# First four chunks normed while modulation blocks load, two attention units made inside the transform, turned head outputs in the head products' bank

## The chip, the cores and the metric

The kernel runs on one core of a Trainium2 chip. The metric is the device time of one execution, in microseconds (us), the median of several. Engines are named as in the profile: TensorE (PE, and PEld for its weight loads), VectorE (DVE), ScalarE (ACT), GpSimd (POOL), and SyncE (SP), which issues all transfers. Each engine works through its own instructions in order; semaphores order them against each other.

## The reference

Two layers of a diffusion backbone on 512 latent and 256 context tokens of width 1024, all in float32. Cut to what matters here:

```python
mod_x = silu(c) @ w_ada[l] + b_ada[l]          # nine vectors of 1024: shift, scale, gate of three sublayers
def ffn_sublayer(s, m, i, g, wg, wu, wd):
    h = rmsnorm(s, g) * (1 + m[3*i+1]) + m[3*i]
    return s + 0.5 * m[3*i+2] * ((silu(h @ wg) * (h @ wu)) @ wd)
# a layer: ffn_sublayer, then token mixing with u = h @ w_in, then ffn_sublayer
p = softmax(q @ k.T / 8)                        # 4 heads, two maps each
o = rmsnorm((p[0] - lam * p[1]) @ v) * const    # differential attention, latent queries see all keys
y = concat(o, conv_module(u), fourier_mix(u)) @ w_out
```

Here conv_module is gated, convolved over 31 tokens, LayerNormed, swished and mapped; fourier_mix is the real part of a 2-D DFT and a linear map. The last layer has no context output.

## The kernel before

**Layout.** Activations stand transposed: eight chunks of 128 channels by 768 tokens. A product is made of three (h_hi with w_hi, h_lo with w_hi, h_hi with w_lo), so each normed chunk h and each weight tile is split into a high part (ScalarE) and a low part (VectorE) before TensorE can use it. PSUM has eight banks. A class Plan numbers every product (slot), gives it a bank, the next in turn unless one is named, and counts each bank's uses; an engine waits for the number of a product, and TensorE (wait_bank, wait_freed) for the count of releases of the bank (bank_free).

**Start.** SyncE loads the tokens, then modulation weights in blocks of 512 columns (load_ada, two halves of 1 MB each), then weight tiles. Block 0 and 1 hold the first shift, 2 and 3 the first scale, for channel chunks 0 to 3 and 4 to 7; 4 and 5 hold the first gate. A block is sixteen matmul records (L1176), a copy by ScalarE (part, L1711), a turn into columns (turn, L1189) and a copy to mod by VectorE (L2157). In `ada(BEFORE)` blocks 0 to 3 come first on each engine, with the turned vectors and the norm's statistics between them. Then shift_scale makes the scales of all chunks and scaled (L2139, tn), high (L1688, h_hi) and low (L2150, h_lo) make the chunks, the context's (segment 1) ahead of the latent ones (segment 0). The up tile is split behind the first context chunk. gate_up_first runs the first group's passes: context gate, context up, blocks 4 and 5 (BETWEEN), then the latent passes.

**Mixing.** After the key, conv, query, value and Fourier projections, `fourier(l)` on TensorE makes the small products of the transform: mean of the convolution (L1451), DFT over positions Z (L1503), variance (L1460), spread of the scales (L1470), DFT over channels F (L1515), Fourier output Fo (L1523) and pointwise output pw (L1482). GpSimd makes the scales (conv_scales) between variance and spread. Fo and pw leave their banks when VectorE has made their low parts (L2710).

**Attention.** Its units are (head, segment, 128 queries): 24 in layer 0 (four latent and two context units a head), 16 latent ones in layer 1. A latent unit takes two of three pairs of banks 0 to 5. In step i TensorE does, in this order: the turn of head output i-9 (turn_o, L1390), the score of unit i (L1558), the first turn of the probabilities of unit i-2 (turn_p, L1572), the head product of unit i-3 (L1584, bank 7), the second turn of probabilities. Turned probabilities and turned head outputs both use bank 6. ScalarE in its step makes the exponents (L2008) and copies turned probabilities (L1994) and head outputs (L2024). VectorE does in step i:

```python
head_low(i - OT_LAG)    # low part of the turned head output, frees its bank
maximum(i)
combine(i - 1)          # the two maps of unit i-1 into one
take_o(i - O_LAG)       # copy of head product i-3 out of bank 7, frees it
```

In three steps each engine also splits a weight tile (1.9 us on ScalarE, 2.3 on VectorE). The last projection (out) follows, and in layer 0 one side product (modulation of a later sublayer) stands behind the first score.

## Time and profile before

| | us |
|---|---|
| median of 3 runs | 2696.61 (2695.8 to 2697.26) |
| the profiled execution | 2699.22 |
| its span, first to last instruction | 2697.4 |
| TensorE busy in it | 2587.2 (96%) |
| VectorE busy | 2079.5 (77%) |
| ScalarE busy | 1020.3 (38%) |
| mean granted TensorE clock, share of full | 0.987 |

TensorE sets the time nearly everywhere. A busy share is an average over stages: the waits by engine and source line tell where TensorE stands idle, and the timelines what it waited for. In a timeline row the columns are start, duration, engine, line, operation, output and inputs, tile shape and count, and in square brackets the idle time ahead of it and what ended it. One fp32 matmul of the start, transform or attention leaves two records.

### The profile page before, as it was taken

Reading aid. Unit: us, or ns where it says so; the run is one execution under the profiler, and the core shown is the slowest. Engines: PE = TensorE matmul, PEld = TensorE weight load, DVE = VectorE, ACT = ScalarE, POOL = GpSimd, SP = SyncE. Lnnn points to the kernel's source line nnn. Section 1 sums busy time; section 2 is a strip of 40 time slices with the busy share of each in tenths; the row PEclk is TensorE's granted clock in tenths of the full one; section 3 lists DMA queues with packets and bytes.
Section 4 is the critical chain, followed back from the end, with each engine's and each line's share of the span. In section 5 each row is a group of like instructions: output and inputs, shape, how many; then the busy total and the mean of one; then the engine's idle time right before and its main releaser. Section 6 shows DMA issues by size and latency. Waiting matters only on the chain. (4 is left out here: it accounts for less than half of the span.)

```text
span 2697.4 us, 42701 instructions
## 1 busy us (share of the span) xinstructions
PE 2587.2 (96%) x15352; PEld 2375.4 (88%) x15352; DVE 2079.5 (77%) x3420; ACT 1020.3 (38%) x1873; POOL 167.6 (6%) x316
## 2 busy tenths in 40 slices
PE   6999999999997999999999999999999987999998
PEld 4899999988955789999999799999997955889997
DVE  5698888888937478888888887777768856688886
ACT  4333432333147333332332434323324155344443
POOL 2000000020003210000000200000001013100001
PEclk7999999999999999999999999999999999999999
DMA  8134333332211112333334133333322211223331
GB/s 304 40 125 130 117 93 115 119 98 63 89 39 48 32 55 89 123 94 113 124 97 133 55 102 117 94 125 108 114 67 89 76 47 32 76 82 110 104 109 53
DMA packets 193241, 256.33 MB, mean 95 GB/s; under 512 B 7262, under 2 KB 130764, under 8 KB 193100
## 3 DMA queue, kind: packets, MB, share of 16 engines
q1 hardware_dynamic: 193100, 254.43, 29.5%
q8 instruction: 91, 1.49, 0.2%
q14 instruction: 50, 0.41, 0.0%
HBM read 252.31 MB, written 2.10 MB: 94 GB/s over the span
## 5 line engine op out<-in xcount | busy, mean ns | idle before, releaser
L1132 PE MATMUL ps<-h_hi,w_hi 128*128 128x384 f32 (+2 forms) x2368 | 792.3, 335 | 21.9 <-DVE h_lo L2150 19.4
L1134 PE MATMUL ps<-h_hi,w_lo 128*128 128x384 f32 (+2 forms) x2368 | 786.8, 332 | 0.0
L1133 PE MATMUL ps<-h_lo,w_hi 128*128 128x384 f32 (+2 forms) x2256 | 750.3, 333 | 0.0
L1132 PEld LDWEIGHTS ps<-h_hi,w_hi 128*128 128x128 f32 x2368 | 450.4, 190 | 54.1 <-issue 21.8
L1134 PEld LDWEIGHTS ps<-h_hi,w_lo 128*128 128x128 f32 x2368 | 450.4, 190 | 20.8
L1133 PEld LDWEIGHTS ps<-h_lo,w_hi 128*128 128x128 f32 x2256 | 429.0, 190 | 19.6 <-issue 1.0
L1663 ACT ACTIVATE w_hi<-raw 128x512 fp32r<-128x512 f32 x464 | 279.8, 626 | 419.1 <-PE ps L1134 325.8
L2282 DVE TENSOR_TENSOR w_lo<-raw,w_hi 128x512 fp32r<-128x512 f32 x464 | 307.3, 684 | 14.7 <-ACT w_hi L1663 14.7
L1132 PE MATMUL ps<-t_hi_all,w_hi 128*128 128x384 f32 x864 | 292.0, 338 | 0.0
L1134 PE MATMUL ps<-t_hi_all,w_lo 128*128 128x384 f32 x864 | 292.0, 338 | 0.0
L1133 PE MATMUL ps<-t_lo_all,w_hi 128*128 128x384 f32 x864 | 291.9, 338 | 0.0
L2205 DVE SCALAR_TENSOR_TENSOR side_acc<-side_raw,ccol,side_acc 128x512 f32<-128x512 f32 x364 | 258.0, 744 | 8.0 <-DMA side_raw<-in_w_ada 8.0
L2400 DVE SCALAR_TENSOR_TENSOR xT<-ps,gate,xT 128x384 f32<-128x384 f32 (+3 forms) x400 | 180.7, 503 | 83.6 <-PE ps L1134 83.4
L1124 POOL TENSOR_TENSOR sqsum<-sqsum,sq 128x256 f32<-128x256 f32 (+1 forms) x98 | 99.1, 1014 | 2027.5 <-ACT sq L1672 2021.0
L1663 ACT ACTIVATE w_hi<-w_sum 128x512 fp32r<-128x512 f32 x216 | 133.4, 626 | 229.3 <-DVE w_sum L866 121.6
L1132 PE MATMUL ps<-even_hi_all,w_hi 128*128 128x384 f32 (+2 forms) x576 | 197.7, 343 | 2.2 <-DVE even_lo_all L2379 2.2
L1134 PE MATMUL ps<-even_hi_all,w_lo 128*128 128x384 f32 (+2 forms) x576 | 195.2, 339 | 0.0
L1133 PE MATMUL ps<-even_lo_all,w_hi 128*128 128x384 f32 (+2 forms) x576 | 194.4, 337 | 0.0
L2282 DVE TENSOR_TENSOR w_lo<-w_sum,w_hi 128x512 fp32r<-128x512 f32 x216 | 147.5, 683 | 19.3 <-ACT w_hi L1663 19.3
L1133 PEld LDWEIGHTS ps<-t_lo_all,w_hi 128*128 128x128 f32 x864 | 162.2, 188 | 0.0
L1132 PEld LDWEIGHTS ps<-t_hi_all,w_hi 128*128 128x128 f32 x864 | 162.2, 188 | 0.0
L1134 PEld LDWEIGHTS ps<-t_hi_all,w_lo 128*128 128x128 f32 x864 | 162.2, 188 | 0.0
(257 smaller groups left out, 4039.5 us busy)
## 6 DMA issues: line engine op xcount, KB each, us to landing
side_raw<-in_w_ada SPq DMA_DIRECT2D x240, 256.0 KB, 2.7
raw<-in_w_ffn_gate SPq DMA_DIRECT2D x44, 1024.0 KB, 5.4
raw<-in_w_ffn_up SPq DMA_DIRECT2D x44, 1024.0 KB, 5.4
raw<-in_w_ffn_down SPq DMA_DIRECT2D x44, 1024.0 KB, 5.0
raw<-in_w_in SPq DMA_DIRECT2D x14, 1024.0 KB, 5.3
ada_buf<-in_w_ada SPq DMA_DIRECT2D x12, 1024.0 KB, 12.7
raw<-in_w_out SPq DMA_DIRECT2D x8, 1024.0 KB, 5.1
raw<-in_w_in SPq DMA_DIRECT2D x8, 512.0 KB, 6.7
```

Source lines behind the costliest of these rows:

```text
L1124: nc.gpsimd.tensor_tensor(sqsum[:, o:o + n], sqsum[:, o:o + n], sq[:, j % 2, o:o + n], ALU.add)\
L1132: mm(out, wh, xh, start=start, stop=False, skip_group_check=reopened)
L1133: mm(out, wh, xl, start=False, stop=False, skip_group_check=reopened)
L1134: return mm(out, wl, xh, start=False, stop=stop, skip_group_check=reopened)
L1663: act_fn(ring_part(w_hi, key(g)), part_source(key(g)), ACT.Copy).then_inc(w_hi_done, 1)
L2205: ins = stt(out=side_acc[:, v, :], in0=side_raw[k % 2][:], scalar=c, in1=side_acc[:, v, :], op0=ALU.mult, op1=ALU.add)
L2282: tt(ring_part(w_lo, key(g)), part_source(key(g)), ring_part(w_hi, key(g)).bitcast(F), ALU.subtract)\
L2400: ins = stt(out=xT[:, j, o:o + n], in0=ps[:, bank_of(key(x)), at_:at_ + n], scalar=gate[:, f // 2, i, j, v:v + 1], in1=xT[:, j, o:o + n], ...
```

## The change

It does three things.

1. **Start.** The blocks come in the order 0, 2, 1, 3. SyncE loads block 0, the constants, the first gate tile, then blocks 2, 1 and 3. TensorE makes block 0, the turned vectors, the statistics and block 2, then the gate passes of the context's chunks 0 to 3, then blocks 1 and 3 with their turns, then the latent chunks 0 to 3. VectorE splits the gate tile ahead of the reciprocals, and makes scales and chunks in two halves (`first_scale`, not shown below: adds the bias to, and makes the scale of, four chunks). The remaining gate passes and the up passes follow in `gate_up_begun`; the up tile is split late, behind latent chunk 5 on ScalarE and behind all chunks on VectorE.
2. **Transform.** Scores 0 and 1 of each layer are products of `fourier(l)`: score 0 and layer 0's side product ahead of the mean, score 1 behind the variance. The transform's other products take turns in banks 4 to 7; both early units use banks 0 to 3. Their maxima, exponents and the first combine move there too. Buffers for probabilities, the scales' diagonals and small columns get other places in SBUF. The attention begins with step 2.
3. **Attention.** Turned head outputs use bank 7, that of the head products, in place of bank 6.

```diff
@@ -74,8 +75,9 @@
-FIRST_BLOCKS = (0, 1, 2, 3, 4, 5)
-BEFORE, BETWEEN = FIRST_BLOCKS[:4], FIRST_BLOCKS[4:]
+FIRST_BLOCKS = (0, 2, 1, 3, 4, 5)
+BETWEEN = FIRST_BLOCKS[4:]
+EARLY = KD // 2
...
@@ -150,7 +152,8 @@
     for i, (h, s, t) in enumerate(units_of(l)):
         mine = [(n + k) % 3 for k in range(2 if s == 0 else 1)]
-        n += len(mine)
+        if i != EARLY_UNITS - 2:
+            n += len(mine)
         out.append((mine, max(busy_until[x] for x in mine)))
...
+    def first_ada(self):
+
+        self.tile(("G", 0, 0))
+        for kind in ("ada", "adaT"):
+            self.slot((kind, 0, 0))
+        for i in range(3):
+            self.slot(("vec", i))
+        for s in seg_order(0):
+            self.slot(("stat", 0, s))
+        for kind in ("ada", "adaT"):
+            self.slot((kind, 0, 2))
+
+        for n, key in enumerate((("ada", 0, 1), ("adaT", 0, 1), ("ada", 0, 3), ("adaT", 0, 3))):
+            self.slot(key, (self.bank + 4 + n) % 8)
...
@@ -330,7 +337,10 @@
+        rest = [(w, f, 0, c, second) for c in range(2) for w in "gu"]
+        if f == 0:
+            passes, rest = [(w, f, 0, c, s) for w in "gu" for s in (first, second) for c in range(2)], []
+        for key in passes + rest:
...
@@ -404,36 +419,43 @@
+        self.before_scores.append(list(self.uses))
+        banks = itertools.cycle(range(4, 8))
+
+        def place(*key):
+            self.slot(key, next(banks))
+
+        self.score(l, 0)
+        if l == MIX_SIDE[0] // 2:
+            place("side", *MIX_SIDE)
...
             if j == 0:
-                self.slot(("var", l))
+                place("var", l)
+                self.score(l, 1)
...
         for kind in ("Fo", "pw"):
             for p in range(2):
                 for s in range(ns):
-                    self.slot((kind, l, p, s))
+                    place(kind, l, p, s)
...
         u = units_of(l)
         self.before_att.append(list(self.uses))
         for i in attention_steps(l):
             if 0 <= i - OT_LAG < len(u):
-                self.slot(("OT", l, i - OT_LAG), 6)
+                self.slot(("OT", l, i - OT_LAG), 7)
             if i < len(u):
-                self.slots[("score", l, i)] = (self.n, None, None)
-                self.n += 1
-            if (l, i) == (0, 0):
-                self.slot(("side",) + MIX_SIDE, 6)
+                self.score(l, i)
...
-            for b in BEFORE[:3]:
+            for b in FIRST_BLOCKS[:1]:
...
             load(("G", 0, 0))
-            for half in range(2):
-                load_ada(3, half)
+            for b in FIRST_BLOCKS[1:4]:
+                for half in range(2):
+                    load_ada(b, half)
...
             def ada(blocks):
+                for b in blocks:
+                    ada_block(b)
+                for b in blocks:
+                    turn(b)
+
+            def first_pass(w, s, ks):
+
+                o, n = PIECES[s][:2]
+                wh, wl = wk((w.upper(), 0, 0), KD)
+                for k in ks:
+                    wait_h(0, k, s)
+                    for c in range(2):
+                        key = (w, 0, 0, c, s)
+                        if k == 0:
+                            wait_bank(pe, key)
+                        last = mm3(pt(key, n), wh[:, k, 128 * c:128 * c + 128], wl[:, k, 128 * c:128 * c + 128],
+                                   h_hi[:, k, o:o + n], h_lo[:, k, o:o + n], k == 0, k == KD - 1, True)
+                        if k == KD - 1:
+                            last.then_inc(products, 1)
+
+            def first_ada():
+                ada_block(0)
+                turn(0)
+                pe.wait_ge(const_landed, 16 * 3)
+                turn_vector(0)
+                turn_vector(1)
+                pe.wait_ge(taps_landed, 16)
+                turn_vector(2)
+                for s in seg_order(0):
+                    stat(0, s)
+                ada_block(2)
+                turn(2)
+                wait_split(("G", 0, 0))
+                first, second = seg_order(0)
+                first_pass("g", first, range(EARLY))
+                ada_block(1)
+                turn(1)
+                ada_block(3)
+                turn(3)
+                first_pass("g", second, range(EARLY))
...
+                def gate_up_begun():
+
+                    for w in "gu":
+                        if w == "u":
+                            wait_split(("U", 0, 0))
+                        for s in seg_order(0):
+                            first_pass(w, s, range(EARLY if w == "g" else 0, KD))
+                            if (w, s) == ("u", seg_order(0)[0]):
+                                ada(BETWEEN)
...
+                for b in range(4):
+
+                    pe.wait_ge(bank_free[b], plan.before_scores[l][b])
+                score(l, 0)
+                if l == MIX_SIDE[0] // 2:
+                    side_product(MIX_SIDE[0], lambda x: x, MIX_SIDE[1])
...
                     if j == 0:
                         conv_var()
+                        score(l, 1)
                 conv_spread()
...
+            def score(l, i):
+
...
-                for b in range(6):
+                for b in (4, 5):
 
                     pe.wait_ge(bank_free[b], plan.before_att[l][b])
...
@@ -2073,16 +2141,29 @@
-            ada(BEFORE)
+            for s, j in square_order(0):
+                square(0, s, j)
+            ada((0,))
+            split(("G", 0, 0))
+            take_vector(0, vcol[:, 0, :])
+            take_vector(1, vcol[:, 1, :])
+            take_vector(2, wdw[:])
+            for s in seg_order(0):
+                root(0, s)
             act.wait_ge(lam_dot, 1)
             act_fn(lamw[:, 0:2 * DEPTH], lamw[:, 0:2 * DEPTH], ACT.Exp).then_inc(lam_exp, 1)
-            high(0, 1, (0,))
+            ada((2,))
+            high(0, 1, range(0, EARLY))
+            high(0, 0, range(0, 1))
+            ada((1,))
+            high(0, 0, range(1, 3))
+            ada((3,))
+            high(0, 0, range(3, EARLY))
+            high(0, 1, range(EARLY, KD))
+            high(0, 0, range(EARLY, 6))
             split(("U", 0, 0))
-            high(0, 1, (1,))
-            high(0, 1, range(2, KD))
-            high(0, 0, range(0, 5))
+            high(0, 0, range(6, KD))
             ada(BETWEEN)
...
-                if l == MIX_SIDE[0]:
+                if l == MIX_SIDE[0] // 2:
                     side_rows(*MIX_SIDE, range(KD))
...
+                maximum(0)
...
+                if l == MIX_SIDE[0] // 2:
+                    side_column(*MIX_SIDE)
+                combine(0)
+                maximum(1)
...
-                for i in range(len(us) + OT_LAG):
+                for i in range(EARLY_UNITS, len(us) + OT_LAG):
                     if 0 <= i - OT_LAG < len(us):
                         head_low(i - OT_LAG)
                     if i < len(us):
                         maximum(i)
-                    if (l, i) == (0, 0):
-                        side_column(*MIX_SIDE)
                     if 1 <= i <= len(us):
                         combine(i - 1)
                     if 0 <= i - O_LAG < len(us):
-            ada(BEFORE)
+            split(("G", 0, 0))
+            over_rms(0, 1)
+            over_rms(0, 0)
+            ada((0, 2))
             for i in range(4):
                 wait_freed(dve, ("vec", i))
-            shift_scale(0, 0)
-            scaled(0, 1, (0, 1))
+            first_scale(0)
+            scaled(0, 1, range(EARLY))
+            scaled(0, 0, range(EARLY))
+            ada((1, 3))
+            first_scale(1)
+            scaled(0, 1, range(EARLY, KD))
+            scaled(0, 0, range(EARLY, KD))
             split(("U", 0, 0))
-            scaled(0, 1, range(2, KD))
-            scaled(0, 0)
             ada(BETWEEN)
```

## Rows read from the trace of the kernel before

**Rows 1.** the page's part 1, TensorE: busy time, share of the span, records

```profile
PE 2587.2 (96%) x15352; PEld 2375.4 (88%) x15352; DVE 2079.5 (77%) x3420; ACT 1020.3 (38%) x1873; POOL 167.6 (6%) x316
```

**Rows 2.** who TensorE waited for over the whole span: total, times, longest

```profile
PE ps L1390 <- ACT pT L1994: 13.3, 22, 0.7
...
PE ps L1572 <- DVE a_lo L2780: 11.4, 15, 1.9
```

**Rows 3.** timeline of TensorE over the start

```profile
27.33 1.93 PE L1176 MATMUL ps<-ada_buf,cpad 128*32 128x512 f32 x8 [7.03 <-DMA ada_buf<-in_w_ada]
...
44.68 1.94 PE L1176 MATMUL ps<-ada_buf,cpad 128*32 128x512 f32 x8 [1.57 <-DMA ada_buf<-in_w_ada]
...
52.88 0.55 PE L1132 MATMUL ps<-h_hi,w_hi 128*128 128x256 f32 x1 [2.76 <-DVE h_lo L2150]
...
69.95 3.64 PE L1176 MATMUL ps<-ada_buf,cpad 128*32 128x512 f32 x32
...
73.52 1.95 PE L1189 MATMUL ps<-sel,part 128*128 128x2 f32 x16
```

**Rows 4.** timeline of VectorE over the start and the first group

```profile
50.16 0.17 DVE L2157 COPY mod<-ps 128x8 f32<-128x8 f32 x1 [1.54 <-PE ps L1189]
...
54.05 2.29 DVE L2123 TENSOR_TENSOR w_lo<-raw,w_hi 128x2048 fp32r<-128x2048 f32 x1 [1.32 <-ACT w_hi L1652]
...
59.92 0.48 DVE L2139 SCALAR_TENSOR_TENSOR tn<-xT,amul,rstd 128x256 f32<-128x256 f32 x1
...
64.63 0.75 DVE L2139 SCALAR_TENSOR_TENSOR tn<-xT,amul,rstd 128x512 f32<-128x512 f32 x1
...
97.49 0.69 DVE L2411 TENSOR_TENSOR even_prod_all<-sil_all,ps 128x512 f32<-128x512 f32 x1 [7.06 <-PE ps L1134]
```

**Rows 5.** timeline of TensorE, end of layer 0's transform and first units

```profile
783.33 5.32 PE L1482 MATMUL ps<-acc,small_tables 128*128 128x512 f32 x16
789.89 1.56 PE L1558 MATMUL ps<-kT,qT 64*128 64x384 f32 x8 [1.25 <-DVE h_lo L2710]
791.38 0.64 PE L1203 MATMUL ps<-side_acc,ones 128*32 128x256 f32 x8
...
797.17 1.61 PE L1558 MATMUL ps<-kT,qT 64*128 64x384 f32 x8 [2.08 <-ACT e L2008]
```

**Rows 6.** timeline of VectorE at the end of that transform

```profile
783.17 2.19 DVE L2710 SCALAR_TENSOR_TENSOR h_lo<-ps,vcol,h_hi 128x512 fp32r<-128x512 f32 x4 [8.37 <-ACT h_hi L1975]
```

**Rows 7.** timeline of TensorE, units 0 and 2 of layer 1

```profile
2191.43 1.56 PE L1558 MATMUL ps<-kT,qT 64*128 64x384 f32 x8 [1.72 <-issue]
...
2198.71 1.56 PE L1558 MATMUL ps<-kT,qT 64*128 64x384 f32 x8 [2.08 <-ACT e L2008]
```

**Rows 8.** busy time in stretches; columns: stretch, its length, five engines, granted clock, DMA, GB/s

```profile
798.60:805.40 6.80, 6.22 (x23) 3.65 (x22) 4.53 (x7) 3.27 (x8) 0.00 (x0) 0.50 0.00 0
825.90:829.30 3.40, 3.40 (x11) 1.74 (x12) 3.11 (x4) 1.01 (x5) 0.00 (x0) 0.50 0.01 4
2228.00:2263.00 35.00, 27.87 (x189) 19.58 (x188) 28.86 (x50) 24.84 (x64) 11.94 (x29) 1.00 0.19 61
```

**Rows 9.** a latent step of layer 1, timelines of TensorE and of VectorE

```profile
2254.21 0.33 PE L1390 MATMUL ps<-ident,onorm 128*128 128x128 f32 x1 [0.58 <-ACT pT L1994]
...
2258.76 0.33 PE L1390 MATMUL ps<-ident,onorm 128*128 128x128 f32 x1 [0.58 <-ACT pT L1994]
...
2256.07 1.82 DVE L2753 TENSOR_REDUCE nb<-ps 128x1 f32<-128x768 f32 x2 [0.40 <-PE ps L1558]
...
2259.25 0.28 DVE L2773 COPY onorm<-ps 128x128 f32<-128x128 f32 x1
```

**Rows 10.** layer 0, turns of head outputs six steps apart; a context maximum

```profile
854.79 0.33 PE L1390 MATMUL ps<-ident,onorm 128*128 128x128 f32 x1 [0.72 <-ACT pT L1994]
...
879.30 0.33 PE L1390 MATMUL ps<-ident,onorm 128*128 128x128 f32 x1 [0.72 <-ACT pT L1994]
...
807.50 0.69 DVE L2756 TENSOR_REDUCE nb<-ps 128x2 f32<-128x512 f32 x1
```

More of the change, by code:

```diff
@@ L420, in mix @@
             for s in range(ns):
[L421 removed]
+                place("F", l, j, s)
         for kind in ("Fo", "pw"):
@@ new lines, in ada_block @@
+            def ada_block(b):
+                key = ("ada", 0, b)
+                wait_bank(pe, key)
+                for k in range(KD):
+                    q, home = k % 4, (b, k // 4)
+                    if k % 4 == 0:
+                        pe.wait_ge(ada_landed[home], 16)
+                    src = ada_buf[home][:].rearrange("p (k n) -> p k n", k=4)
+                    last = mm(ps[32 * q:32 * q + 32, bank_of(key), :], cpad[:, k, :], src[:, q, :],
+                              start=(k < 4), stop=(k >= 4), skip_group_check=True)
+                last.then_inc(products, 1)
@@ L1526, in fourier @@
                 point_wise()
+            def score(l, i):
+                h, s, t = units_of(l)[i]
+                mine, need = score_slots(l)[i]
+                if t == 0 and s == 0:
+                    pe.wait_ge(q_ready, HEADS * l + h + 1)
+                    pe.wait_ge(k_ready, HEADS * l + h + 1)
+                    wait_freed(pe, ("K", l, h, 1))
+                if need:
+                    pe.wait_ge(exp_done, 2 * units_before(l) + need)
+                o = mix_segs(l)[s][0] + 128 * t
+                if s == 0:
+                    parts = [(st, 2 * mine[st] + half, 384 * half, 384) for half in range(2) for st in range(2)]
+                else:
+                    parts = [(st, 2 * mine[0] + st, LAT, CTX) for st in range(2)]
+                for st, b, ko, n in parts:
+                    r = slice(64 * st, 64 * st + 64)
+                    last = mm(ps[:, b, 0:n], qT[r, h, o:o + 128], kT[r, h, ko:ko + n],
+                              start=True, stop=True, skip_group_check=True)
+                last.then_inc(products, 1)
             def attention(l):
                 us = units_of(l)
-                ms = mix_segs(l)
                 u_before = units_before(l)
-                e_before = 2 * u_before
-                slots = score_slots(l)
-                for b in range(6):
+                for b in (4, 5):
                     pe.wait_ge(bank_free[b], plan.before_att[l][b])
@@ L1940, in mix @@
                     copy(("X", l, t), xN[:, t, :], 256)
+                for st in range(2):
+                    exponent(0, st)
                 def copy_z(j):
@@ L1956, in mix @@
                 act_fn(cvar[:, 0:nt], pt(key, nt), ACT.Identity, bias=epsc[:], scale=1.0 / CONVW).then_inc(bank_free[bank_of(key)], 1)
+                for st in range(2):
+                    exponent(1, st)
                 copy_z(1)
@@ L2176, in shift_scale, with first_scale @@
                              in1=vcol[:, l, g0:g0 + KD], op0=ALU.add, op1=ALU.mult))
+                settle()
+            def first_scale(h):
+                x = slice(EARLY * h, EARLY * h + EARLY)
+                y = slice(KD + EARLY * h, KD + EARLY * h + EARLY)
+                for m in (x, y):
+                    for v in range(2):
+                        step(tt(mod[:, 0, m, v], mod[:, 0, m, v], vcol[:, 0, m], ALU.add))
+                settle()
+                g0 = ROW["g_ffn1"][0] + EARLY * h
+                for v in range(2):
+                    step(stt(out=amul[:, 0, 0, x, v], in0=mod[:, 0, y, v], scalar=1.0,
+                             in1=vcol[:, 0, g0:g0 + EARLY], op0=ALU.add, op1=ALU.mult))
                 settle()
@@ L2712, in biased_low, with maximum, combine @@
                         .then_inc(bank_free[bank_of(key)], 1)
+                def maximum(i):
+                    h, s, t = us[i]
+                    wait_products(dve, ("score", l, i))
+                    p, mine = i % 2, score_slots(l)[i][0]
+                    if s == 0:
+                        for st in range(2):
+                            dve_.reduce_max(nb[:, p, st:st + 1], ps[:, 2 * mine[st]:2 * mine[st] + 2, 0:384], AX.XY,
+                                            negate=True).then_inc(max_done, 1)
+                    else:
+                        dve_.reduce_max(nb[:, p, :], ps[:, 2 * mine[0]:2 * mine[0] + 2, 0:CTX], AX.X,
+                                        negate=True).then_inc(max_done, 1)
+                def combine(i):
+                    h, s, t = us[i]
+                    dve.wait_ge(exp_done, 2 * (u_before + i + 1))
+                    c, n = ratio[:, i % 8:i % 8 + 1], TOK if s == 0 else CTX
+                    step(dve_.reciprocal(rs[:, i % 2, 1:2], esum[:, i % 16, 1:2]))
+                    settle()
+                    step(dve_.tensor_scalar(c, rs[:, i % 2, 1:2], esum[:, i % 16, 0:1], neglam[:, l:l + 1], ALU.mult, ALU.mult))
+                    settle()
+                    stt(out=e0[i % 3][:, 0:n], in0=e1[i % 2][:, 0:n], scalar=c, in1=e0[i % 3][:, 0:n],
+                        op0=ALU.mult, op1=ALU.add).then_inc(p_ready, 1)
+                maximum(0)
                 for s, (o, n) in enumerate(ms):
```

219 lines of the change are left out of this document (70 added, 149 removed).

## The prediction

> **What bounds the kernel now.** I read the page first: TensorE is busy almost throughout [rows 1], so only its idle time, and time at its lower clock level, can be won. TensorE's waits [rows 2], the timelines of the three stretches that the change touches, and the granted clock then say where those lie. They are (a) everything ahead of the first gate products, (b) the start of each layer's attention, (c) the waits within the attention for the bank 6 in which probabilities and head outputs are both turned.
>
> **Part A, the first chunks.** Modulation blocks arrive in a row: the first half of block 1 at 27.33, the second half of block 3 at 44.68, six megabytes later [rows 3], so 2.9 us each. Before, nothing can be normed until block 3 is there; the first gate product is at 52.88 [rows 3]. Chunks 0 to 3 need blocks 0 and 2 alone. The new order is gate tile, block 2, block 1, block 3, so block 2 is complete two megabytes after 27.33, at 33.1. The way from a last half block to the first product took 52.88 - 44.68 = 8.2, which puts the first product at 41.3. Block 3's own arrival does not move, and all of chunks 4 to 7 hangs on it. It now also stands behind other TensorE work: the context's first pass (24 products), block 1 and its turn.
>
> A product of 512 columns: from the end of the turns (73.52 + 1.95 = 75.47) to VectorE's last product multiply (97.49) there are 96 [rows 3, 4], so 0.23 each; 256 columns half of it, the lower clock level twice it. The stretch 41.3 on starts at the lower level: 24 x 0.23 = 5.5 if it stays there, 4.3 if it rises near the end; to 45.6. A block of sixteen products with the turn of one block, from 69.95 to 75.47 for two [rows 3], is 2.8, and a copy of 0.7 between the two is not hidden any more: 3.5. Block 1 and block 3: to 52.6. From block 3's modulation at VectorE (50.16 before) to the first product were 2.7 [rows 3, 4], here to 55.3 for context chunk 4. VectorE then makes four context chunks at 2 x 0.48 less overlap, 0.92, and four latent ones at 2 x 0.75, 1.46 [rows 4]: about 9.2 with what is pipelined, to 64; the up tile's high part, now between latent chunks 5 and 6 on ScalarE, adds about 0.8, and its low part 2.29 [rows 4]: up products from 67.2. TensorE has by then done the other gate passes (24 x 0.23 + 24 x 0.12 + 24 x 0.23 = 13.9 from 52.6: 66.5), so VectorE's split is last by little. Then 48 context products 5.8, blocks 4 and 5 with turns 5.6, 0.4 for VectorE's copies (the latent up products now reuse these banks), 48 latent products 11.0: 90.0. Before, this point was 97.4 [rows 4]. **Part A: -7.4**, between -2 (first pass and both blocks wholly at the lower level, 5.4 more) and -9. What follows is fed by weights that are issued earlier too, and I find no transfer that becomes last. The extra order on ScalarE costs an activation table load ahead of block 2's copy; it lies under VectorE's reciprocals.
>
> The Trainium skill, "ScalarE: Activation LUTs", section "What ACT_TABLE_LOAD costs", adds a drain to every switch of table set and so gives 2.66 us. No run here shows the drain; at that price block 2's copy would be 1.4 later and part A some 0.6 less.
>
> **Part B, two units in the transform.** Before, layer 0's units 0, 1 and 2 start at 789.89, some 793.5 and 797.17: each score waits for the exponent of the unit before [rows 5]. Now units 0 and 1 and the side product are TensorE work within the transform, and unit 2 stands where unit 0 stood. Moved work: 2 x 1.49 and 0.55 for the side product (789.89 to 791.38 is one unit's pitch) [rows 5]. Their maxima and exponents fall where VectorE and ScalarE mostly wait. Saved: 7.28 - 2.98 - 0.55 = 3.75. Against it: the transform now has four banks, so layer 0's first pointwise product needs the bank of the first Fourier output, whose low part starts at 783.17 and, as the first and longest of four in 2.19, takes some 0.7, while the product ran at 783.33 [rows 5, 6]: a stall of 0.65 with its signal. Layer 0: -3.1. Layer 1 has half as many products, none of them meets a bank in use: 2198.71 - 2191.43 - 2.98 = -4.3 [rows 7]. After unit 2 layer 0 lost more, for TensorE was on its lower level from 798.6 to 805.4 [rows 8]; with 3.5 less idle ahead of it I expect the upper level: 1.6 more. **Part B: -9.0**, between -4 (half of it eaten by ScalarE's new exponents ahead of squares and copies) and -10.
>
> **Part C, head outputs turned in bank 7.** It removes the wait of the turn for the copied probabilities (13.3 in all) and of the probabilities for the released head output (11.4) [rows 2]. It adds two. The head output's turn for step i now needs bank 7 as head product i-4 left it, and VectorE copies that one last in its step i-1, behind the maximum and the combine. Behind the waiting turn, in TensorE's order, stands the score, which VectorE's next maximum waits for. So a ring closes: turn, score, maximum, combine, copy, turn. From a turn at 2254.21 the copy starts at 2259.25 and takes 0.28; with the signal the next turn is at 2259.6, a pitch of 5.39, where now it is 2258.76 - 2254.21 = 4.55 [rows 9]. Before, the copy was off the path. **Each latent step after a latent one costs +0.84.** Layer 1 has seven such steps (units 9 to 15). Where VectorE or ScalarE also splits a weight tile, the step was already longer and the ring adds 0.6 to 1.2. Step by step I get +3.7 up to unit 15; in the last three steps, without scores, the copy is early and 2.3 come back, but the last head product then waits 1.1 for its bank's head output: +2.5 in layer 1.
>
> In layer 0 the steps differ. A context step has a maximum of 0.69 [rows 10] instead of 1.82 [rows 9] and a score of half the matmuls, 0.8 less: its ring is 3.4. Behind a context unit the combine has a third of the elements, an estimated 0.5 less (0.2 to 0.7): a latent step is 4.85 there, a context step 3.2, which is TensorE's own work. One head of six steps: 4.85 + 3 x 5.39 + 3.4 + 3.2 = 27.6; before, turn to turn from 854.79 to 879.30, 24.5 [rows 10]: +3.1. The six steps before 854.79 have splits and a low stretch [rows 8] and so less to lose, +1.7 by the same count; the tail +0.1: +4.9 if no step falls to the lower level. I add 1.5, one such stretch, since the ring leaves 5.39 - 3.97 = 1.42 idle in each step (3.97: the pitch of 4.55 less its wait of 0.58) [rows 9]. **Part C: +8.9**, between +4 and +14; below that only if the ring isn't there (a rival below).
>
> By the Trainium skill, "TensorE: Matmul & The Clock Gate", section "HAM oscillation — how this bites in real kernels", waits as short as these, between work of more than their length, should leave the clock alone; by that rule the 1.5 would be zero. But the stretch from 798.6 on ran at 0.50 behind waits of 2.08 and less [rows 5, 8], so here row and rule differ, and I keep the 1.5.
>
> **Sum**: -7.4 - 9.0 + 8.9 = -7.5. The profiled execution took 2699.22 (span 2697.4, 1.8 around it), 2.6 above the median of 2696.61. So 2691.7 profiled, **2689.1** at the median.
>
> **Rivals.** (1) Part C gives its waits back: if VectorE's copy came before the turn wants it, 12 to 24 of the 24.7 [rows 2] would go: -16.4 - 15 or so, 2665. For it: these are the largest waits. Against: VectorE's order is not changed, and the row at 2259.25 is later than the turn at 2258.76. (2) The first stretch stays on the lower clock, blocks 1 and 3 included: part A is -2, 2694.5. For it: eight records took 1.93 at 27.33 and 1.94 at 44.68, twice what 32 in 3.64 give [rows 3]; against: a dense first pass is now ahead of the blocks. (3) **Slower**: the ring's idle time drops TensorE to the lower level in the attention. At that level a turn and its score take 1.75 more, all on the ring. 22 steps have both. The sum without my 1.5 is -9.0, so it decides from six steps on (9.0 / 1.75); in half of them it is 11 x 1.75 - 9.0 = +10, 2707. For: [rows 8]. Against: layer 1 kept the upper level through its own waits [rows 8]. (4) The change doesn't do what it says: the early units stall the transform by what they save (squares, variance and scales late), part B about 0, 2698. Against: VectorE sat idle for 8.37 just there [rows 6], and scales were not late.
>
> **How the numbers follow.** Forecast 0.58, own range 2684 to 2693; rival 1 0.12, rival 2 0.13, rival 3 0.08, rival 4 0.09. The range leaves out no more than rivals 1 and 3, 0.20, and keeps what of rival 1 is a part only: 2672 to 2698. A measurement of this kernel can tell 0.2%, 5.4 us, from no change. Faster by more than that: 0.50 of the forecast, rival 1, nothing of rival 2: 0.62. Slower: rival 3 and the worst of 4: 0.10. The rest, 0.28, is within.
>
> **What would show it.** A: first gate product near 41, the up products from 67, the last group-0 multiply near 90 in place of 97.49. B: units 0 and 1 between the side product and the pointwise products, a stall near 0.6 ahead of the latter in layer 0 and none in layer 1; unit 2 directly behind the transform. C: TensorE's wait list has head output turns behind VectorE's copy of head products instead of behind ScalarE's copy, and latent steps at 5.4. Wrong if steps stay at 4.5 or below, or if blocks 1 and 3 end after 56.

## The result, and the profile after

| | before | after |
|---|---|---|
| median of nine runs on one chip | 2698.80 us | 2704.03 us |
| lowest, highest | 2695.80, 2701.58 | 2703.30, 2709.44 |
| profiled execution, its span | 2699.22, 2697.4 | 2703.80, 2702.0 |
| TensorE busy | 2587.2 | 2591.1 |

The ratio is 1.0025, with a 95% interval of 1.0016 to 1.0033: the change costs 0.25%, some 6 us. The prediction was 7.5 us (0.3%) faster, and 2704.03 lies above its range.

TensorE's busy time on the page of the changed kernel is 4 higher though its products are the same, as [rows 1] showed it before:

```profile
PE 2591.1 (96%) x15352; PEld 2376.4 (88%) x15352; DVE 2080.9 (77%) x3428; ACT 1023.4 (38%) x1875; POOL 167.0 (6%) x316
```

Who TensorE waited for, changed kernel (total, times, longest). L1460 is the turn of a head output, L1660 the head product, L1624 the score, L1648 the turn of probabilities, L1552 the pointwise product:

```profile
PE ps L1460 <- DVE onorm L2869: 28.2, 23, 2.7
...
PE ps L1660 <- DVE a_lo L2876: 7.1, 11, 1.9
...
PE ps L1624 <- ACT e L2024: 6.1, 6, 1.8
PE ps L1648 <- ACT pT L2010: 4.6, 8, 1.0
...
PE ps L1552 <- DVE h_lo L2801: 0.5, 1, 0.5
```

The first line is new: the 13.3 for the copied probabilities [rows 2] are gone, the turns wait 28.2 for VectorE's copy of head products instead. Of the 11.4 for VectorE's low halves, which free the bank, 7.1 are left (second line), now ahead of the head product. Together that is 10.6 more than the 24.7 before. The last line is the bank stall that the prediction put at 0.65.

Where the two traces part, read from the timelines of TensorE (starts in us):

| point | before | after | difference |
|---|---|---|---|
| first gate product | 52.88 | 39.93 | -13.0 |
| VectorE's last multiply of group 0 | 97.49 | 89.9 | -7.6 |
| score of layer 0's unit 2 | 797.17 | 788.84 | -8.3 |
| turn of head output 0 | 825.53 | 817.36 | -8.2 |
| turn of head output 6 | 854.79 | 850.38 | -4.4 |
| turn of head output 12 | 879.30 | 881.00 | +1.7 |
| first product of layer 0's output projection | 897.85 | 902.66 | +4.8 |
| score of layer 1's unit 2 | 2198.71 | 2198.37 | -0.3 |
| turn of its head output 0 | 2227.84 | 2228.86 | +1.0 |
| turn of its head output 7 | 2263.30 | 2267.87 | +4.6 |
| span | 2697.4 | 2702.0 | +4.6 |

So the start gave what it should, and layer 0's attention lost 13.0 between head output 0 and the output projection, where +4.9 had been forecast, with 1.5 for the clock on top. Layer 1's lost 3.6 up to head output 7, and gave 0.7 of it back.

The start, TensorE, then VectorE:

```profile
39.93 0.55 PE L1160 MATMUL ps<-h_hi,w_hi 128*128 128x256 f32 x1 [2.65 <-DVE h_lo L2231]
...
45.26 1.92 PE L1194 MATMUL ps<-ada_buf,cpad 128*32 128x512 f32 x16
...
48.88 1.92 PE L1194 MATMUL ps<-ada_buf,cpad 128*32 128x512 f32 x16
```

```profile
89.33 1.28 DVE L2502 TENSOR_TENSOR even_prod_all<-sil_all,ps 128x512 f32<-128x512 f32 x2
```

The row holds the last two multiplies, which start at 89.3 and 89.9; before, the last stood alone at 97.49 [rows 4]. The first product of the context's chunks was forecast for 41.3 and came at 39.93. Its pass ran at the lower clock level to its end (24 products in 5.33, from 39.93 to 45.26); modulation blocks 1 and 3 take 1.92 for sixteen records, the upper clock level (eight took 1.93 in [rows 3]).

A latent step of layer 1, TensorE and then VectorE, to be held against [rows 9]:

```profile
2257.12 0.33 PE L1460 MATMUL ps<-ident,onorm 128*128 128x128 f32 x1 [1.42 <-DVE onorm L2869]
2257.38 1.56 PE L1624 MATMUL ps<-kT,qT 64*128 64x384 f32 x8
...
2259.25 1.50 PE L1660 MATMUL ps<-vN,pT 128*128 128x128 f32 x12
2260.59 0.49 PE L1648 MATMUL ps<-ident,e 128*128 128x128 f32 x3
2262.50 0.33 PE L1460 MATMUL ps<-ident,onorm 128*128 128x128 f32 x1 [1.41 <-DVE onorm L2869]
```

```profile
2258.99 1.82 DVE L2811 TENSOR_REDUCE nb<-ps 128x1 f32<-128x768 f32 x2 [0.75 <-PE ps L1624]
...
2261.22 1.02 DVE L2825 SCALAR_TENSOR_TENSOR e<-e,ratio,e 128x768 f32<-128x768 f32 x1
2262.16 0.28 DVE L2869 COPY onorm<-ps 128x128 f32<-128x128 f32 x1
```

From turn to turn 5.38, where 5.39 was forecast. TensorE is through with its own work at 2261.08 and waits 1.41 for the copy at 2262.16, which is last behind maximum and combine.

The same ring in layer 0, TensorE, one step ahead of the costliest and that one:

```profile
838.25 0.33 PE L1460 MATMUL ps<-ident,onorm 128*128 128x128 f32 x1 [1.16 <-DVE onorm L2869]
...
840.00 0.44 PE L1648 MATMUL ps<-ident,e 128*128 128x128 f32 x2
840.27 0.61 PE L1660 MATMUL ps<-vN,pT 128*128 128x128 f32 x4
843.63 0.33 PE L1460 MATMUL ps<-ident,onorm 128*128 128x128 f32 x1 [2.75 <-DVE onorm L2869]
843.89 2.93 PE L1624 MATMUL ps<-kT,qT 64*128 64x384 f32 x8
...
847.36 0.61 PE L1660 MATMUL ps<-vN,pT 128*128 128x128 f32 x4
...
850.38 0.33 PE L1460 MATMUL ps<-ident,onorm 128*128 128x128 f32 x1 [1.73 <-DVE onorm L2869]
```

Here units of the context lie among those whose head products are due: four records in 0.61 at 840.27, not twelve in 1.50, and two turned blocks, not six. The pitch is still the ring's 5.38 (838.25 to 843.63), so TensorE idles 2.75 of it. And then the score at 843.89 takes 2.93 in place of 1.56: the lower clock level. The step from 843.63 to 850.38 is 6.75 long. The granted clock (the number behind the five busy times, 0.86 and 1.00) in layer 0's ring and in the whole of layer 1's attention:

```profile
840.00:890.00 50.00, 36.90 (x201) 23.88 (x200) 31.34 (x65) 28.00 (x81) 10.07 (x36) 0.86 0.00 0
2228.00:2275.00 47.00, 34.19 (x229) 24.11 (x228) 33.52 (x60) 31.05 (x81) 16.47 (x38) 1.00 0.15 45
```

### The profile page after: what moved, and what is told of

It is laid out like the page before. It is cut to its first block and busy times, and to the rows that moved or that the text cites. A ratio compares the mean times of both kernels' runs of the same rounds, so it can differ in the third digit from the quotient of the medians.

```text
span 2702.0 us, 42746 instructions
## 1 busy us (share of the span) xinstructions
PE 2591.1 (96%) x15352; PEld 2376.4 (88%) x15352; DVE 2080.9 (77%) x3428; ACT 1023.4 (38%) x1875; POOL 167.0 (6%) x316
```

## The experiments

A, B and C are the parts of the prediction: start, transform, attention. Each kernel was timed, in five to twelve runs, against the kernel before on one chip. Medians of kernels of different groups compare by their ratios. The mean granted clock is that over all timed runs.

| kernel | what it is | median us | ratio, 95% interval | mean clock |
|---|---|---|---|---|
| start_alone | part A | 2691.16 | 0.9975 (0.9965 to 0.9984) | 0.990 |
| units_alone | part B | 2691.94 | 0.9971 (0.9959 to 0.9983) | 0.989 |
| bank7_alone | part C | 2717.23 | 1.0070 (1.0054 to 1.0086) | 0.984 |
| bank6 | A and B | 2685.49 | 0.9946 (0.9934 to 0.9959) | 0.992 |
| the changed kernel | A, B and C | 2704.03 | 1.0025 (1.0016 to 1.0033) | 0.987 |
| copy_first | A, B, C, copy ahead of combine | 2682.70 | 0.9939 (0.9926 to 0.9952) | 0.992 |
| score_first | A, B, C, score ahead of the turn | 2692.25 | 0.9978 (0.9968 to 0.9987) | 0.989 |
| filled | A, B, C, waits filled | 2703.04 | 1.0016 (1.0006 to 1.0025) | 0.992 |
| filled_half | the same, less | 2701.47 | 1.0013 (1.0004 to 1.0022) | 0.990 |
| table_early | copy_first, table loaded early | 2683.17 | 0.9941 (0.9927 to 0.9954) | 0.991 |
| bank6_table | A, B, table loaded early | 2684.66 | 0.9947 (0.9933 to 0.9961) | 0.990 |
| tail6 | copy_first, last turns in bank 6 | 2684.64 | 0.9946 (0.9933 to 0.9960) | 0.991 |
| together | all repairs | 2679.71 | 0.9927 (0.9913 to 0.9941) | 0.992 |

The kernel before has 0.987 to 0.988. In us, a ratio is worth its distance from 1 times 2699.

### Each part by itself

```diff
-                self.slot(("OT", l, i - OT_LAG), 7)
+                self.slot(("OT", l, i - OT_LAG), 6)
```

That line makes bank6 out of the changed kernel; the reverse on the kernel before makes bank7_alone. start_alone and units_alone are the kernel before with the hunks of part A or of part B (that with bank 6).

> Part C undone alone: parts A and B stay, head outputs are turned in bank 6 again. Theory 1 (the ring through bank 7, with the lower clock that it brings, is what costs): the two traces stand 8.2 us apart at layer 0's first turn of a head output (825.53 before, 817.36 after), and layer 1's own part B is worth 3.0 net up to its first turn; nothing is lost behind either, so 11 us under the kernel before, give or take 3, and no wait for the copy of head products. Theory 2 (the early units are what costs: they bring an activation table load and a low-clock stretch into places where nothing hides them, and the ring is only a wait that moved): no more than 4 us under the kernel before.

> Part C alone on the kernel before. Theory 1: its cost on record was 8.9 us; the trace of the changed kernel has two steps in a head of layer 0 at 6.75 instead of 5.39, and layer 1 loses 4.2, so I now expect +12 to +18 us over the kernel before, latent steps of 5.4, the same wait list as the changed kernel. Theory 2: the ring only moves waits, so +4 us or less.

> Part A alone on the kernel before. If what the trace shows at the last multiply of the first group (89.33 against 97.49) is kept to the end, -7 to -8 us (7.1 are still there at layer 0's transform). If later weights or the clock take it back, -3 us or less.

> Part B alone on the kernel before, head outputs in bank 6. My sum on record was -9.0. The traces so far say: -1.3 at layer 0's unit 2 (a low-clock stretch inside the transform takes 1.8 of the 3.1), nothing more up to the first turn (the table load of 1.28 against the low-clock pair behind unit 2), -4.2 at layer 1's unit 2, +1.2 from the table load there: -5 in all, and the medians with and without part B on top of part A stand 5.7 apart. Expected: 5 to 7 us under the kernel before. If parts A and B do not add up (part B only pays with part A's shift): 3 or less.

Part A: -6.7 (4.3 to 9.4 less). Part B: -7.8 (4.6 to 11.1 less). A and B together: -14.6. Part C: **+18.9** (14.6 to 23.2 more), twice its forecast of +8.9. The three add up to +4.4, and the changed kernel has +6.7 (4.3 to 8.9 more): nothing beyond the intervals says that they disturb each other. With bank 6 the ring is gone and the old wait is back as it was, to be read against the first row of [rows 2]:

```profile
PE ps L1460 <- ACT pT L2010: 13.3, 22, 0.7
```

So theory 1 holds, and by more than it said: bank7_alone was to cost 12 to 18 and cost 18.9, and bank6 was to gain 8 to 14 and gained 14.6. units_alone too gained more than the 5 to 7 expected.

### The ring, broken in two ways

```diff
+                    if 0 <= i - O_LAG < len(us):
+                        take_o(i - O_LAG)
                     if 1 <= i <= len(us):
                         combine(i - 1)
-                    if 0 <= i - O_LAG < len(us):
-                        take_o(i - O_LAG)
```

> The changed kernel, with VectorE's copy of the head product moved ahead of its combine (behind the maximum), no wait and no work changed. Theory 1: the turn in bank 7 then waits for a copy that ends at about the maximum's end plus 0.3, where TensorE is itself still turning probabilities, so latent steps of layer 1 fall from 5.38 to 4.0 to 4.5, the low-clock stretches of layer 0's attention become fewer, and the kernel beats both: 10 to 20 us under the kernel before. Theory 2 (steps are held by something else, so the wait changes its name): steps stay at 5.2 or more and the time within 3 us of the changed kernel.

VectorE's maximum, copy and combine in layer 1, copy_first:

```profile
2244.45 1.81 DVE L2811 TENSOR_REDUCE nb<-ps 128x1 f32<-128x768 f32 x2
2246.30 0.29 DVE L2869 COPY onorm<-ps 128x128 f32<-128x128 f32 x1
...
2247.00 1.02 DVE L2825 SCALAR_TENSOR_TENSOR e<-e,ratio,e 128x768 f32<-128x768 f32 x1
```

Two turns of head outputs next to each other, same kernel, TensorE:

```profile
2246.64 0.33 PE L1460 MATMUL ps<-ident,onorm 128*128 128x128 f32 x1
...
2250.74 0.33 PE L1460 MATMUL ps<-ident,onorm 128*128 128x128 f32 x1
```

The copy now starts at 2246.30, right behind the maximum; the next turn stands at 2246.64 and waits for nothing. The pitch is 4.10, less than the 4.55 of before and 1.28 less than the ring's. The kernel is 16.5 faster than before (ratio 0.9939), 23 ahead of the changed kernel by the ratios, for two calls that changed places. In its trace layer 0's attention has the upper clock from 800 to 887.

That is the ring's price given back, and little more. Against bank6, which has no part C at all, the ratios leave 2 us (0.9939 and 0.9946, with intervals that overlap). TensorE's waits in copy_first say why:

```profile
PE ps L1660 <- DVE a_lo L2876: 10.6, 9, 1.7
PE ps L1648 <- DVE e L2825: 9.0, 12, 1.2
...
PE ps L1460 <- DVE onorm L2869: 5.2, 8, 1.3
```

These are 24.8 in all, as much as the 24.7 of [rows 2] that part C took away: the turned probabilities now wait for the combine, which the copy has pushed back. A head of layer 0 takes 23.7 (head outputs 6 to 12) where it took 24.5, but from head output 12 to the output projection it is 20.0 where it was 18.6, in part for a low stretch from 887.4 to 894.3.

In score_first it is TensorE's order that is turned round, with the plan's counting to match:

```diff
-                    if 0 <= i - OT_LAG < len(us):
-                        turn_o(l, i - OT_LAG)
                     if i < len(us):
                         score(l, i)
+                    if 0 <= i - OT_LAG < len(us):
+                        turn_o(l, i - OT_LAG)
```

> The changed kernel with TensorE's order in a step turned round: the score ahead of the head output's turn, so that no score stands behind a turn that waits for the copy. If the ring is turn, score, maximum, combine, copy, the maximum can now start when VectorE is free; but VectorE's low half of the head output, ahead of the maximum, waits for the turn, which now ends later. Worked out for layer 1: turn at 0, high half 0.3 to 0.6, low half to 0.9, maximum to 2.8, combine to 4.4, copy to 4.7, next turn 4.9: a pitch of 4.9 to 5.1 in place of 5.38, so the ring gets shorter by the part of the score that is not hidden and is not broken: 3 to 8 us under the changed kernel. Rival (the score's place has nothing to do with it): 5.38 as before.

Turns of TensorE, then VectorE's copy (L2869) and low half (L2876), layer 1:

```profile
2241.57 0.33 PE L1460 MATMUL ps<-ident,onorm 128*128 128x128 f32 x1
...
2246.16 0.33 PE L1460 MATMUL ps<-ident,onorm 128*128 128x128 f32 x1
```

```profile
2241.18 0.28 DVE L2869 COPY onorm<-ps 128x128 f32<-128x128 f32 x1
2242.34 0.35 DVE L2876 SCALAR_TENSOR_TENSOR a_lo<-ps,gsub,h_hi 128x128 fp32r<-128x128 f32 x1 [0.88 <-ACT h_hi L2040]
...
2245.77 0.28 DVE L2869 COPY onorm<-ps 128x128 f32<-128x128 f32 x1
```

The pitch is 4.59, not 4.9 to 5.1. Each link came a little earlier than I had it: from a turn at 2241.57 the low half starts 0.77 later, the next copy 4.20 later (2245.77) and takes 0.28, the next turn is there at 4.59. The kernel gained 12.7 on the changed one, more than the 3 to 8 expected, for layer 0's ring from 840 on had no low clock stretch either. (Layer 1 had two, from 2233.0 and 2256.9, though its longest waits just ahead of them were 1.92 and 1.37.) The rival (5.38 as before) is out: what made the ring long was the score behind the waiting turn.

### Is it the clock?

In filled_half and filled, TensorE makes throw-away products ahead of some of layer 0's head products, into the bank region that the head product overwrites. Nothing is left out.

```diff
+FILL = {9: 4, 10: 7, 11: 4, 12: 4, 15: 4, 16: 7, 17: 4, 18: 4}
...
                         ks = range(6) if s == 0 else range(4, 6)
+                        for _ in range(FILL.get(u, 0) if l == 0 else 0):
+                            mm(ps[:, 7, 0:128], pT[:, u % 2, 0, :], vN[:, ks[0], 128 * h:128 * h + 128],
+                               start=True, stop=True, skip_group_check=True)
```

In filled the numbers were 6 to 15, at ten units (5, 6, 9 to 12 and 15 to 18).

> The changed kernel with extra products in layer 0's attention: ahead of ten head products TensorE makes 6 to 15 throw-away products of 128 columns into the bank that the head product then overwrites (nothing is left out, the result is the same). They fill most of the 1.2 to 2.7 us in which TensorE waits for the copy and end before it does, so the ring keeps its pace. Theory 1 (the idle time of the ring drops TensorE's clock, and that is most of what my sum for part C lacked): the five low stretches between 840 and 905 go down to two or fewer, steps of 6.7 become 5.4, and the time falls by 3 to 6 us under the changed kernel, though work was added. Theory 2 (the low stretches come from something else, or the extra products only lengthen the ring): steps and time as in the changed kernel or longer.

> The filled kernel with fewer throw-away products: 7 where TensorE waits 2.7 us, 4 (1.0 us) elsewhere, eight steps in all. In the filled kernel all low stretches between 840 and 905 went, but one throw-away product took 0.25, twice what I had reckoned, so that TensorE's own work set steps of 5.6 to 6.4. Theory 1 (idle time of the ring drops the clock): steps of these eight at 5.4, at most two low stretches left, so 3 to 6 us under the changed kernel. If half the filling is too little to keep the clock: low stretches as in the changed kernel and its time.

TensorE in filled_half, one step, L1661 being the throw-away products (eight records, for four products):

```profile
843.02 0.33 PE L1461 MATMUL ps<-ident,onorm 128*128 128x128 f32 x1 [1.18 <-DVE onorm L2873]
...
845.15 1.06 PE L1661 MATMUL ps<-vN,pT 128*128 128x128 f32 x8
846.05 0.61 PE L1664 MATMUL ps<-vN,pT 128*128 128x128 f32 x4
846.49 0.49 PE L1649 MATMUL ps<-ident,e 128*128 128x128 f32 x3
848.40 0.33 PE L1461 MATMUL ps<-ident,onorm 128*128 128x128 f32 x1 [1.41 <-DVE onorm L2873]
```

Layer 0's ring in filled_half, then in filled; the changed kernel's 0.86 for the same stretch stands above:

```profile
840.00:890.00 50.00, 41.91 (x295) 31.07 (x294) 33.91 (x72) 31.76 (x92) 11.93 (x45) 1.00 0.00 1
```

```profile
840.00:890.00 50.00, 46.83 (x347) 36.92 (x344) 31.35 (x64) 27.81 (x80) 9.98 (x36) 1.00 0.00 1
```

Both have a granted clock of 1.00 where the changed kernel has 0.86 with four low stretches of 3.4 us each (from 843.8, 850.7, 874.6 and 881.4). In filled_half seven of the eight filled steps are 5.37 to 5.39 long (the eighth, behind a context unit, 4.84), and from the start of the ring to the output projection the trace lost 8.4 instead of 13.0 against the kernel before (9.1 ahead at head output 0, 0.7 ahead at the first output product). The changed kernel's step of 6.75 less 5.38 is the price of a low stretch there: 1.37. So the added work made layer 0's attention faster, by 4.6 in the trace. Of that 2.4 are left in the whole span (2699.6 against 2702.0), which has low stretches elsewhere. The ratios of the times, 1.0025 and 1.0013, are 3 us apart with intervals that overlap, so the gain of the whole kernel is not resolved. What is shown is the clock: over all timed runs its mean rises from 0.987 to 0.990 and, in filled, 0.992. The kernel filled was expected to be 3 to 6 us under the changed kernel and came out 2 under it. It went too far: one product costs 0.22 (fifteen in 3.35), so the head products and the copies behind them came so late that steps grew to 6.37, which ate what the clock gave.

### The table load, and the last steps

```diff
                         biased("pw", "b_pw", 4, p, s)
+                act_fn(ojunk[:, 0, 0:1], epsc[:], ACT.Exp)
```

> The kernel with the copy first, and one exponent of a single column on ScalarE behind the last pointwise product's bias, so that the activation table of the exponents is loaded there, while ScalarE waits, and not behind unit 2's maximum. Theory (the early units put a table load of 1.28 us on the path of each layer, which my sum for part B lacked): unit 3's score waits 0.5 instead of 1.76 in both layers, -2.6 us under the kernel with the copy first. Rival (the wait for unit 2's exponent is the bank rotation's, not the table's): the wait stays at 1.7 and the time is the same.

> Parts A and B without part C, and the exponents' table loaded early as before. Against bank6 it prices the table load again: -2.6 us, 2683. Against the kernel with all four repairs it prices what bank 7 is worth once its copy is early: 2 to 4 us.

In the changed kernel, layer 1, unit 2 and unit 3 of TensorE, and the load between on ScalarE:

```profile
2198.37 1.56 PE L1624 MATMUL ps<-kT,qT 64*128 64x384 f32 x8 [1.56 <-DVE h_lo L2801]
...
2203.29 1.56 PE L1624 MATMUL ps<-kT,qT 64*128 64x384 f32 x8 [1.76 <-ACT e L2024]
```

```profile
2200.95 1.28 ACT L2024 ACT_TABLE_LOAD   x1
```

The same in table_early:

```profile
2182.19 1.56 PE L1624 MATMUL ps<-kT,qT 64*128 64x384 f32 x8 [1.56 <-DVE h_lo L2802]
...
2185.83 1.56 PE L1624 MATMUL ps<-kT,qT 64*128 64x384 f32 x8 [0.48 <-ACT e L2024]
```

```profile
2181.37 1.28 ACT L2093 ACT_TABLE_LOAD   x1
```

Unit 3's score waits 0.48 instead of 1.76: 1.28 a layer, the length of the load, and the same in layer 0 (0.47 instead of 1.75). From unit 2 to head output 0 the traces of bank6 and bank6_table differ by 1.3 in each of the two layers. The rival is out. The timed medians don't resolve 2.6: 2683.17 against 2682.70, and 2684.66 against 2685.49.

tail6 puts the turns of the three steps without a score back into bank 6 (`7 if i < len(u) else 6`).

> The kernel with the copy first, and the three turns of head outputs behind the last score in bank 6 again. In those steps there is no score and no maximum, so bank 7 has nothing to give and the last head product waits for its release by the turned output (0.94) with TensorE mostly idle, behind which the clock fell (887 to 894). Expected: -3 to -4 us in layer 0 with the low stretches there gone, -1 us in layer 1. If the clock falls there all the same: -1.5 us in all.

Measured by the trace, from head output 14 to the output projection: 1.3 less than copy_first (10.6 against 11.9), whose clock fell at 887 and did not here. In layer 1, from head output 6 on, it is 0.2 less (14.35 against 14.57), since the first turn in bank 6 waits again. Expected were 3 to 4 and 1. The medians don't show it (2684.64 against 2682.70): **not resolved** by time. In together the copy is also behind the combine in context steps.

> Copy first, table early and the last three turns in bank 6 together, and in steps that score a context unit the copy stays behind the combine (its maximum is 0.7 long, so the ring is 3.4 there and the copy first would hold the combine back: turned probabilities wait 0.56 for it). Expected: 2.6 + 4 us under the kernel with the copy first, another 1 to 2 for the context steps (3.4 to 3.5 instead of 3.9 to 4.0): 2676, 23 under the kernel before, if the clock keeps up.

It gave 2679.71, ratio 0.9927: 19.7 under the kernel before and 26 under the changed kernel, but 3.7 short of the 2676 expected. Most of the steps of 3.94 stayed; that last edit made one step 0.27 shorter and another 0.18 longer in each head. Against bank6_table, which has A, B and the early load but no part C, together is 5 us ahead by the ratios (0.9927 and 0.9947, intervals that overlap): what bank 7 is worth at best.

## Why the prediction was wrong

Forecast and measurement, -7.5 and +6.7, are 14 us apart. Part C is 10 of it, A and B are 0.7 and 1.2, and the rest lies in how the three add up.

**Part A (-7.4): right.** Measured -6.7 alone, -7.6 in the trace at the end of group 0 (89.9, forecast 90.0). Blocks 1 and 3 ran at the upper level; rival 2 is out.

**Part B (-9.0): direction and mechanism right, 1 us too much.** Measured -7.8 alone. Counted from the transform's start, layer 1's unit 2 came 4.2 earlier in the traces of units_alone and of bank6, forecast 4.3. Layer 0's came 2.9 earlier in units_alone, forecast 3.1; in the changed kernel only 1.2, for a low stretch fell on the transform. Not in the sum: the load of the exponents' table, which the early exponents split from the rest by silu, square and identity, and which the old order hid in the wait ahead of unit 0. It is 1.28 a layer. The 1.6 for a better clock behind unit 2 did come, and covers layer 0's load.

**Part C (+8.9): the step that failed, by 10 us.** The ring itself was right: its links, its pitch (5.38 for 5.39) and the sum for a head: 27.6 was forecast for six steps, and filled_half has 28.3 from head output 6 to 12 (5.38, 3.81, 3.50, 4.85, 5.38, 5.38), 0.4 of it from its fill. What failed is the sum around it: two of its terms were too small.

- **The clock**, 1.5, from "the ring leaves 5.39 - 3.97 = 1.42 idle in each step". That idle time holds for steps whose units are all latent. In a step TensorE scores one unit, turns the probabilities of the unit two before it and makes the head product of the one three before it. Around each change of head in layer 0 the latter two are context units while a latent maximum still sets the ring's length. There the wait is 2.75, longer than the work of 2.63. The changed kernel fell to the lower level right behind it at both such places, each time for two steps, and again where the output projection begins (from 901.8); bank7_alone did so from 852.3, 859.1 and 883.0, and for 6.8 from 906.9. In these two kernels the steps of layer 1 wait 1.4 and kept 1.00.
- **The steps of layer 0 outside the counted head**, 1.7 and 0.1. Read from filled_half, less its fill: 2.7 up to head output 6 (1.7 forecast) and 1.5 behind head output 12 (0.1 forecast), where each head product waits until VectorE has the low half of the turned output, 0.76, 0.72 and 0.94 in a row in the changed kernel. I had counted that wait for layer 1 alone. A head is 3.4 (3.1), layer 1 is 2.9 in bank7_alone (2.5).

So the ring by itself is 2.7 + 3.4 + 1.5 + 2.9 = 10.5 where my terms without the clock made 7.4. In the changed kernel the rest is seen directly: layer 0's attention lost 13.0, of which the ring is 7.6, and four low stretches at 1.37 are the other 5.4. For part C alone, the other 8.4 of the 18.9 are the clock's only by difference, some 7 of the 10 that I missed. The mean clocks agree: 0.984 against 0.988 over all runs is, by an estimate (twice the difference times 2700), some 20 us more at half the clock, or six stretches of 3.4, where I had one. Its one trace shows less: three stretches that cost 3.1 in layer 0's attention and 2.1 lost between there and layer 1's, in a run 16.7 longer than the kernel before.

The dense work behind the last waits then starts at the lower level, here in bank7_alone (the stretch of the first output products):

```profile
906.90:913.70 6.80, 5.86 (x17) 4.71 (x17) 0.64 (x2) 0.66 (x3) 0.00 (x0) 0.50 0.00 0
```

**The rivals.** Rival 3 named the mechanism that did it, gave it 0.08, and asked for six of 22 steps at 1.75. In truth it was four steps at 1.37 and the entry into the output projection. It was too cheap because I looked at layer 1 for evidence against, where idle time is half. Rival 1 is out, here and for copy_first as well: with the copy early, the waits of [rows 2] went and others of the same length took their place, so some 2 us came back of the 12 to 24 that it named. Rival 4 is out.

The rows of layer 1 (a wait of 1.41 in a step of 5.38, clock 1.00) and of layer 0 (2.75 in 5.38, clock down) lie on two sides. The Trainium skill, "TensorE: Matmul & The Clock Gate", section "HAM oscillation — how this bites in real kernels", describes the drop for bursts of work that are shorter than the wait behind them, which fits both; its own example has waits of 3 to 5 us, and here 2.75 was enough. I had applied that rule to the mean of the steps. The row that I set against it, the stretch from 798.6, stands behind scores of 1.56 with waits of 2.08, so it is no evidence against it. Nor does the wait decide alone. The same scores with the same waits of 2.08 ran at 1.00 in layer 1 of the kernel before (2191.4 to 2200.3) and in layer 0 of start_alone (782.0 to 790.9). And the kernel before and start_alone, without any ring, have low stretches in the attention too, from 839.5 and from 829.1.

**Open.** A low stretch stands right behind the variance's 24 products of one column in the changed kernel, TensorE:

```profile
755.46 2.73 PE L1530 MATMUL ps<-ones,csq 128*128 128x1 f32 x24
758.12 2.60 PE L1624 MATMUL ps<-kT,qT 64*128 64x384 f32 x8
```

So does one in eight of the ten other kernels with part B in them, and in bank7_alone, which has no early unit. In the changed kernel it costs 1.0 on that score and 0.6 on what follows. In units_alone the same order runs at the upper level:

```profile
762.37 2.73 PE L1478 MATMUL ps<-ones,csq 128*128 128x1 f32 x24
765.03 1.56 PE L1572 MATMUL ps<-kT,qT 64*128 64x384 f32 x8
```

What decides between the two was not found, nor why repeated runs of one kernel differ: bank7_alone's six go from 2713.21 at a mean clock of 0.988 to 2723.50 at 0.980. In most kernels the spread of the runs follows the granted clock closely, so that a difference of 3 us or less was read from traces here.

## What to carry to other kernels

When a buffer is reused one step later, write down the ring of waits that closes through it, and look for the link that waits only by its place in an engine's order: here two calls that changed places on VectorE turned +6.7 into -16.5. Then compare with the kernel without the idea: undoing part C gave -14.6, so nearly all of that is parts A and B, and a wait that is removed can come back under another name. Work out TensorE's idle time for each kind of step, not for the mean one: here the clock fell behind the waits of 2.75 and not behind those of 1.4, and its price came on top of the wait. A moved activation takes its table load along; see where the table is switched back.

## What the runs showed of the hardware

Throw-away products, 0.22 us each for fp32 of 128 columns, kept TensorE's granted clock at 1.00 from 840 to 890, through steps with 0.4 to 1.4 of idle time left, where it had been 0.86 on average, and layer 0's attention was 4.6 faster with them than without (for the whole kernel the gain is not resolved). And a low stretch of 3.4 us cost 1.37 in an attention step that has waits, though it doubles the time of each product in it, since part of the step's idle time takes it up.
